# Re-ordering VectorE and GpSimd in the output loop of a mixer with routing

## What is computed

```python
out = concatenate([y_lru, y_ret], -1) @ w_out        # y_ret = head_rms(o) * silu(g)
x = x + g1 * out
h = modulate(rmsnorm(x), sh2, sc2)                   # h = x * rstd * a2 + b2
s = sigmoid(h @ w_router); sb = s + b_router
gidx = top_k(sum of the 2 best of each group, 4)
eidx = top_k(where(group chosen, sb, -inf), 6)
gates = s[eidx] / sum(s[eidx]) * 2.5
x = x + g2 * (routed experts + shared expert)
```

## Time and profile before

| | |
|---|---|
| median of 3 runs | 2626.4 us (2625.27 to 2628.41) |
| profiled execution, span | 2626.2 us |
| mean granted TensorE clock, whole span | 0.977 of full |
| TensorE matmul busy, whole span | 94% |
| VectorE / ScalarE / POOL busy, whole span | 66% / 39% / 37% |
| steps with routing in the output loop, 967.2 to 1087.7 us | 120.5 us: TensorE 111.72, VectorE 82.35, ScalarE 31.45, POOL 89.19 us busy, clock 1.00 |

### The profile page before, as it was taken

One profiled execution on the slowest core, in us unless ns is written; L12 is line 12 of the kernel. 1 busy time (PEld: TensorE's weight loads), 2 busy tenths in 40 slices (PEclk: granted clock), 3 DMA queues, 4 the chain that ended last, 5 costly groups with the idle time before them and its releaser, 6 DMA issues. The chain is left out here.

```text
span 2626.2 us, 47471 instructions
## 1 busy us (share of the span) xinstructions
PE 2475.5 (94%) x11959; PEld 2018.1 (77%) x11960; DVE 1723.1 (66%) x2748; ACT 1015.2 (39%) x1623; POOL 970.1 (37%) x1001
## 2 busy tenths in 40 slices
PE   7999999998989999779999999999999999999996
PEld 4788777776767888657888888878788787887875
DVE  4763674557345666775578586877857778587855
ACT  2321433333422222213345353555534455354633
POOL 1211016642153677742333333343333333333321
PEclk9999999999989999979999999999999999999998
DMA  7776686856766556348689798998979989799874
GB/s 293 270 284 230 226 288 239 279 210 233 289 239 238 191 189 199 127 142 261 155 271 276 188 303 257 267 321 242 302 209 273 295 239 313 201 303 308 275 233 180
DMA packets 241222, 645.79 MB, mean 246 GB/s; under 512 B 24172, under 2 KB 37808, under 8 KB 225008
## 3 DMA queue, kind: packets, MB, share of 16 engines
q1 hardware_dynamic: 191856, 467.62, 49.7%
q0 software_dynamic: 49280, 177.08, 26.6%
HBM read 470.43 MB, written 174.18 MB: 245 GB/s over the span
## 5 line engine op out<-in xcount | busy, mean ns | idle before, releaser
L2601 PE MATMUL ps_h<-shared,x_exp_t_hi 128*128 (+1 forms) x2432 | 589.0, 395 | 24.5 <-ACT x_exp_t_hi L2342 11.9
L2601 PEld LDWEIGHTS ps_h<-shared,x_exp_t_hi 128*128 128x128 f32 x2432 | 462.9, 191 | 126.4 <-issue 14.7
L2235 POOL DMA_INDIRECT sum_d<-w_shared_raw,small_cols x136 | 235.4, 1731 | 609.0 <-DMA sum_d<-w_shared_raw,small_cols 276.3
L1218 PE MATMUL ps_p<-shared 128*128 128x512 f32 x1632 | 390.9, 397 | 7.0 <-DVE kvqg_out L107 3.2
L2601 PE MATMUL ps_y<-shared,h_exp_t_hi 128*128 (+1 forms) x1216 | 346.3, 407 | 27.7 <-DVE h_exp_t_lo L2398 25.4
L1218 PEld LDWEIGHTS ps_p<-shared 128*128 128x128 f32 x1632 | 307.3, 189 | 75.8 <-DVE kvqg_out L107 4.1
L2372 DVE TENSOR_TENSOR shared<-w_exp,shared (+1 forms) x260 | 311.7, 1220 | 11.0 <-ACT shared L2280 5.1
L2601 PE MATMUL ps_h<-shared,x_exp_t_lo 128*128 (+1 forms) x1216 | 318.6, 404 | 0.0
L2312 ACT ACTIVATE h_exp_t_hi<-ps_ht 128x256 fp32r<-128x256 f32 x152 | 58.3, 384 | 614.8 <-PE ps_ht L2610 608.8
L2601 PEld LDWEIGHTS ps_y<-shared,h_exp_t_hi 128*128 128x128 f32 x1216 | 221.9, 192 | 74.1 <-issue 24.0
L2280 ACT ACTIVATE shared<-w_exp (+1 forms) x260 | 260.1, 1057 | 41.6 <-DMA w_exp<-in_experts 39.1
(11 more groups left out here) (305 smaller groups left out, 3571.5 us busy)
## 6 DMA issues: line engine op xcount, KB each, us to landing
w_exp<-in_experts SPq DMA_DIRECT2D x390, 512.0 KB
shared<-hx_d SPq DMA_DIRECT2D x58, 1024.0 KB, 6.2
shared<-rec_d SPq DMA_DIRECT2D x16, 1536.0 KB
shared_raw<-in_w_mod_rest POOLq DMA_DIRECT2D x16, 1024.0 KB, 5.8
rec_d<-shared_raw SPq DMA_DIRECT2D x48, 256.0 KB, 4.8
rec_d<-kvqg_out SPq DMA_DIRECT2D x48, 256.0 KB, 4.5
hx_d<-shared SPq DMA_DIRECT2D x10, 1024.0 KB, 6.2
xt<-in_xt POOLq DMA_DIRECT2D x18, 512.0 KB, 8.7
```

What stands on the lines that cost most here:

```text
L1218: last = pe.matmul(ps_p[:, s % 2], hx0[:, at, x, k].bitcast(F32R), wa[w][:, k, p % 2 * HD:(p % 2 + 1) * HD].bitcast(F32R), start=(m + k == ...
L2235: pool.indirect_dma_start(sum_d[:, :], bass.IndirectOffsetOnAxis(give[:, par:par + 1], 0), y[:, par], None, compute_op=ALU.add).then_inc(a ...
L2601: last = pe.matmul(out, x[:, j * P:(j + 1) * P].bitcast(F32R), w_part[:, bass.ds(w_at + j * stride, 512)].bitcast(F32R), start=(start and ...
```

## The change

VectorE: `choose` ends after the indices (L1356). Its last two operations become a function `mark`, called behind y. `gates` of a tile moves from the end of a step to the next step, behind qf. ScalarE: the tanh waits for the first operation of the choice of the tile before, not for `chosen`, and the second half of `scores` is issued later, behind the high half of yl. POOL: the order becomes rh, rstd, then qb and the state of the next tile, then b2 for h of tile n-1 (in the step before the one that it was in), then `enlist`. TensorE and SyncE are unchanged.

```diff
-    N_TOP, N_CHOICE = 18, 14
+    N_TOP, N_PICK, N_CHOICE = 18, 13, 14
...
     tops.of(dve.tensor_copy(R.f8[:], R.i8[:]))
+    assert tops.n == R.N_PICK
+
+
+def mark(dve, R, t, b):
+
+    tops = Count(dve, R.top_own, t * R.N_TOP + R.N_PICK)
     each = [P, TOP_K, N_EXP]
     tops.of(dve.tensor_tensor(R.eq6[:, b], R.iota[:, None, :].broadcast_to(each),
                               R.f8[:, 0:TOP_K, None].broadcast_to(each), ALU.is_equal))
     wait_over_zero(dve, R.rank_done, t)
     dve.tensor_reduce(R.chosen[:], R.eq6[:, b].rearrange("p j e -> p e j"), AX.X, ALU.add).then_inc(R.chosen_done, 1)
...
 POOL, step(n, par)
-                if on(n, 2):
-                    t = n - 2
-                    pool.wait_ge(h2s_done, t + 1)
-                    pool.tensor_tensor(h2[:, par], h2[:, par], b2[:], ALU.add).then_inc(h2_done, 1)
-                if on(n, 0):
-                    pool.wait_ge(qt_copied, n + 1)
-                    wait(pool, o_done, n)
-                    pool.tensor_tensor(qb_t[:], q_t[:], xi[:, 1], ALU.mult).then_inc(qb_done, 1)
...
                     pool.tensor_tensor(rstd[:, b], rstd[:, b], mhalf[:], ALU.pow).then_inc(rstd_done, 1)
+                if on(n, -1):
+                    m, at_m = n + 1, 1 - par
+                    pool.wait_ge(qt_copied, m + 1)
+                    wait(pool, o_done, m)
+                    pool.tensor_tensor(qb_t[:], q_t[:], xi[:, 1], ALU.mult).then_inc(qb_done, 1)
+                    wait(pool, sf_done, m)
+                    pool.tensor_tensor(sfd[:].rearrange("p (h e) -> p h e", h=HEADS),
+                                       sfs[at_m].rearrange("p (h e) -> p h e", h=HEADS),
+                                       gc[:, :, None].broadcast_to([P, HEADS, DH]), ALU.mult).then_inc(sfd_done, 1)
+                    pool.wait_ge(sfd_done, m + 1)
+                    pool.wait_ge(rec_loaded[at_m], (half(m, at_m) + 1) * 16)
+                    pool.tensor_tensor(sfs[1 - at_m], sfd[:], rec[at_m][:, 2 * HD:3 * HD], ALU.add).then_inc(sf_done, 1)
...
+                if on(n, 1):
+                    t = n - 1
+                    pool.wait_ge(h2s_done, t + 1)
+                    pool.tensor_tensor(h2[:, 1 - par], h2[:, 1 - par], b2[:], ALU.add).then_inc(h2_done, 1)
                 if on(n, 4) and n <= NT:
                     enlist(pool, R, n - 4, par, list_d)
...
 ScalarE
+            def tanh_of(t):
+
+                act.wait_ge(r_done, t + 1)
+                if t > 0:
+                    act.wait_ge(R.top_own, (t - 1) * R.N_TOP + 1)
+                act.activation(th[:], ps_s[:, 0:N_EXP], ACT.Tanh, scale=0.5).then_inc(th_done, 1)
+
             def scores(t):
 
-                act.wait_ge(r_done, t + 1)
-                wait(act, R.chosen_done, t)
-                act.activation(th[:], ps_s[:, 0:N_EXP], ACT.Tanh, scale=0.5).then_inc(th_done, 1)
                 wait(act, entry_done, t)
...
                 if on(n, 3):
-                    scores(n - 3)
+                    tanh_of(n - 3)
...
                     act.activation(yl[0][:, par].bitcast(F32R), yl_raw[:, par], ACT.Copy).then_inc(yl_hi, 1)
+                if on(n, 3):
+                    scores(n - 3)
...
 VectorE, step(n, par)
                     dve.tensor_tensor(qf_t[:], ps_q[:], xi[:, 0], ALU.mult).then_inc(qf_done, 1)
+                if on(n, 4):
+                    gates(dve, R, n - 4, par)
...
                     last.then_inc(y_done, 1)
                 if on(n, 3):
-                    gates(dve, R, n - 3, 1 - par)
+                    mark(dve, R, n - 3, 1 - par)
                 if isinstance(n, int) and n == NT + 1:
+                    gates(dve, R, NT - 2, 1 - par)
                     place(dve, R, NT - 2, 1 - par, ps_q)
```

More of the change, by code:

```diff
@@ L1361, in choose @@
     dve.tensor_reduce(R.chosen[:], R.eq6[:, b].rearrange("p j e -> p e j"), AX.X, ALU.add).then_inc(R.chosen_done, 1)
-    assert tops.n == R.N_CHOICE
+    assert tops.n == R.N_CHOICE - R.N_PICK
 def gates(dve, R, t, b):
@@ L1398, in place, with enlist @@
     dve.tensor_copy(R.slot_u[:, b], R.slot[:]).then_inc(R.slot_done, 1)
[L1401 to L1407, removed]
+def enlist(pool, R, t, b, list_d, places=range(TOP_K)):
+    if 0 in places:
+        pool.wait_ge(R.entry_done, t + 1)
+        pool.tensor_copy(R.entry[:, b, :, 0], R.token[:, bass.ds(t, 1)].broadcast_to([P, TOP_K])).then_inc(R.listed_ids, 1)
+        pool.wait_ge(R.listed_ids, t + 1)
+        wait_apart(pool, R.slot_done, t + 1)
+    for j in places:
         pool.indirect_dma_start(list_d[:, :], bass.IndirectOffsetOnAxis(R.slot_u[:, b, j:j + 1], 0),
@@ L1596, in step @@
                     pool.tensor_tensor(rstd[:, b], rstd[:, b], mhalf[:], ALU.pow).then_inc(rstd_done, 1)
+                if on(n, -1):
[10 more added lines that the diff above has]
+                    pool.tensor_tensor(sfs[1 - at_m], sfd[:], rec[at_m][:, 2 * HD:3 * HD], ALU.add).then_inc(sf_done, 1)
+                if n == 1:
+                    pool.wait_ge(rows_loaded, 16 * N_ROWS)
+                    pool.wait_ge(c_loaded, 16 * N_CONST)
+                if on(n, 1):
+                    t = n - 1
+                    pool.wait_ge(h2s_done, t + 1)
+                    pool.tensor_tensor(h2[:, 1 - par], h2[:, 1 - par], b2[:], ALU.add).then_inc(h2_done, 1)
                 if on(n, 4) and n <= NT:
@@ L1663, in step @@
                 if n == NT + 1:
+                    tanh_of(NT - 1)
                     scores(NT - 1)
@@ L2505, in after @@
                     choose(dve, R, NT - 1, 1)
+                    mark(dve, R, NT - 1, 1)
                     gates(dve, R, NT - 1, 1)
```

## The result

The kernel after takes **2653.2 us** (median of 4 runs, 2649.7 to 2654.1) against 2625.8 (4 runs beside it): 1.0098 times as long, 95% interval 1.0085 to 1.0112. The prediction was 2641, +14.4 us, with the range to 2650. Direction and ring came as written; the size was 13 us short of the measured +27.4.

What follows compares the result with a forecast made beforehand. TensorE was taken as the bound before, a ring through GpSimd's list writes after. Eleven closings at 1.51 us give 16.6, plus 0.5 ahead, minus 1.8 and 0.9 at the end: +14.4 us, 2641, range 2623 to 2650.

Steps and rivals of the forecast that it cites:

- The ring: Steady steps: rh, y, marks, qf, gates, h2s, h2add, list writes, next rh close a chain; 21.85 us per step, 1.51 more.
- place's product at the second write: VectorE's product in place falls beside the second list write's start in each step; between 0 and 0.4, taken as 0.25 us.
- Both hold-ups: In each step L1358 (marks) starts 0.92 us late behind qb, the gates' first product 0.73 late behind the state.
- A: The forecast itself: the POOL ring with both hold-ups, shift 12 to 19 us, 2638 to 2646; chance 0.62.
- B: Ring closes without one hold-up (2632, chance 0.10) or without both (2620, or 2623 with the writes' 0.25; chance 0.11).
- Ahead of the ring: Before rh(4): rank(0) stands behind the delayed marks and qf; +0.5 us, between 0 and 0.9.
- y behind rh(15): End of the steady steps: y(15) starts 1.36 us after rh(15) instead of 3.14; -1.8 us.
- h2add(15): Tail: h2add, now ahead of the writes, follows h2s directly; a gain of 1.2 us, of which 0.9 is counted.
- the tail behind h2add(15): From h2add(15) on: no cost was entered; the stages behind this one were said only to start later.
- C: POOL does not bind and both TensorE waits shrink as meant; some 14 us less, 2612; chance 0.05.
- D: Choice's and place's casts and small scalings and the list writes hold each other; 0.8 us a step, +9, 2650; chance 0.08.
- E: Longer TensorE waits lower its granted clock; a tenth of the stage's 224 us, +20 more, 2660; chance 0.04.

Runs made afterwards that it cites:

- ids_ahead: Kernel after with the copy of the token numbers ahead of h's addition on GpSimd, the writes still behind it: 2636.9 us, 1.0034 of before.
- split: Kernel after with three of the six list writes ahead of h's addition and three behind it: 2622.0 us, 0.9979 of before.
- small_both: Kernel after with GpSimd's two state operations and qb cut to four columns from tile 2 on (output wrong): 2654.6 us, 1.0099 of before.
- tail: Kernel after with tile 12's six writes ahead of h's addition in the last full step only: 2644.0 us, 1.0072 of before.
- ve_only: Kernel after with GpSimd's old order, so only VectorE's and ScalarE's part of the change: 2619.0 us, 0.9972 of before.
- h2_last: Kernel after with h's addition behind the six list writes instead of ahead of them: 2677.5 us, 1.0186 of before.
- pool_only: Kernel before with GpSimd's new order and nothing else of the change: 2668.3 us, 1.0159 of before.
- late_qb: Kernel after with GpSimd's qb and state waiting until VectorE's gates are done: 2662.2 us, 1.0130 of before.
- late_ids: ids_ahead with GpSimd's qb and state waiting until VectorE's gates are done: 2670.2 us, 1.0154 of before.
- ve_tail: ve_only with four writes ahead of h's addition in the last step and two behind it: 2616.6 us, 0.9959 of before.
- ports: Kernel after with GpSimd waiting for the marks before qb: 2659.3 us, 1.0120 of before.
- small_state: Kernel after with GpSimd's two state operations cut to four columns from tile 2 on, qb whole (output wrong): 2665.1 us, 1.0145 of before.

## Why the prediction was right in its mechanism and short in its size

- **The ring**: right. 22.00 us per step against 21.85; every station agrees within 0.05 us up to h2s. Of the 0.15 more, 0.12 is place's product at the second write, costed at 0.25 and measured at 0.37 (0.96 to 1.33). ids_ahead and split show that it is a ring and not a coincidence. 11 steps make +18.3 against +16.6.
- **Both hold-ups** (A against B): present, 1.43 and 1.29 us in each step, and 1.61 us of the ring by small_both for the 1.65 costed; the margin of 0.2 us held. The Trainium skill, SBUF — State Buffer (Who interferes with whom), had them as an exclusive lock; the durations agree.
- **Ahead of the ring**: +1.3 for +0.5, and +0.4 in tail with the same code, so the term isn't refuted. **y behind rh(15)**: -1.7 for -1.8.
- **h2add(15)**: the step "with h2add ahead of the writes it follows h2s directly" came true, and TensorE's wait fell from 6.20 to 4.14 us, but y(15) to h2add(15) grew by 0.5 where 0.9 was to be gained. The 0.9 us by which h2s(15) was to end later is there (1.0 in ve_only, split and h2_last); the other 1.5 is TensorE's granted clock, which fell to its lower level in the last full step of after. The prediction asked for the clock only in the steady steps.
- **The step that failed is the tail behind h2add(15)**, costed at nothing beyond that gain and measured at +6.2. With the six writes back ahead of h2add (tail) it is 0.0. The prediction moved six writes behind h2add and asked what they hold up on GpSimd alone. It did not follow their landing: the gates of tile 14 reuse the buffer, and the stage's end waits for GpSimd's queue. In the steady steps the same wait doesn't show. Together with the row above the tail is 7.6 us off, the ring 1.7, the start 0.8: 10.1 of the 11.4 us that the profiled spans (+25.8) miss. The rest lies outside the stage, where the same code differs by as much between profiles. The medians lie another 1.6 us apart (+27.4), which no profile places.
- **Rivals**: C (GpSimd doesn't bind) fell, rh had no idle ahead of it. D fell, the mean of a write stayed near 1.0. E fell in the steps of this kernel, came in its last one for 1.5 us, and came in the steps of its relatives, beside late squares that no rival had. Its price, a tenth of the stage, had no row behind it.
- The reading "VectorE's order is what could be gained" was sound as to its direction: ve_only gains 8.5 us.

## What to carry to other kernels

When an operation is queued ahead of another on an in-order engine, write out who feeds it and who waits for what is now behind it, until the chain closes or leaves the step; a closed chain is added up in full and compared with the step. Do the same once more for the last steps, with TensorE's clock and with the landing of the DMAs that moved: a reused buffer and the end of a stage wait for them there, though the steady steps hide it. Slack ahead of an engine's wait is the place for its independent work: here qb and the state fit into the idle time ahead of rh (ve_only, 19.6 us a step) and the step took 5 us more when they stood behind it with the same order of writes and h2add (h2_last, 24.9).

## What was not expected of the hardware

- A stage ended either 10.26 us behind GpSimd's last list write or 3.87 us behind VectorE's last operation, whichever was later, in 13 of 14 profiles: 10.26 in after, pool_only, split, ids_ahead, late_qb, late_ids and the two small ones; 3.87 behind VectorE (and 13.01 behind h2add) in before, ve_only, h2_last and tail, and 3.86 in ve_tail. ports fits neither: 10.51 behind the write, 4.96 behind VectorE.
- An indirect write of 128 entries of 8 bytes costs GpSimd 1.26 to 1.27 us where nothing lengthens it (0.96 and 0.30 to the next; the first of six takes 1.07), and in after the last of six was seen by VectorE 2.6 us behind its end.
- A scaling of 128x6 took 1.28 us instead of 0.23 beside a GpSimd addition (ports): a small operation is held for about as long as the addition itself takes.
- ScalarE's squares, which wait for TensorE's signal, started 2 to 5 us behind the last recorded product of o in most steps of ports, late_qb, late_ids, small_state and small_both and in five steps of pool_only (1.4 in five more); 0.75 in split, and 0.0 in the other kernels.
- TensorE's granted clock stayed at 1.00 in after's steps with waits of 1.8 and 1.3 us in each, and fell to the lower level in the last full step behind waits of 2.2 and 0.7.
